# Sample keys of the stick-breaking attention: 14 of 32 unit products moved from VectorE to GpSimd

## The chip, the cores and the metric

The kernel runs on one core of one Trainium2 chip. The metric is the device time of one execution in microseconds (us), lower is better. Engines are named TensorE (PE in the profile), VectorE (DVE), ScalarE (ACT), GpSimd (POOL) and SyncE (SP).

## The reference

One step of one hybrid decoder layer, for a prompt of 256 tokens and 8 sample tokens (one token for each of 8 sequences, each with 2048 tokens of paged past), all in float32, width 1024. The change touches one product of it: the sample queries of the stick-breaking attention with the past keys.

```
def _stick_breaking(q, k, v, q_pos):
    z = jnp.einsum('bqhd,bshd->bhqs', q, k).astype(jnp.float32) * HEAD_DIM ** -0.5
    strict = (jnp.arange(L)[None, :] < q_pos[:, None])[None, None]
    log_keep = jnp.where(strict, jax.nn.log_sigmoid(-z), 0.0)
    after = lax.cumsum(log_keep, axis=3, reverse=True) - log_keep
    a = jnp.where(strict, jnp.exp(jax.nn.log_sigmoid(z) + after), 0.0)
    o = jnp.einsum('bhqs,bshd->bqhd', a, v)
```

Here b is one of 8 samples, h one of 8 heads, s one of 2048 past positions, d one of 64 dimensions. Beside it runs a sparse attention (for each query the best 256 keys by an indexer's score, then softmax), then projections, gates, and a mixture of 32 experts.

## The kernel before, in words

The first third of the program is a mixture of four streams, each written out by hand in the order of one engine's queue; semaphores tie them together.

The key product. The 2048 past keys of a sample are cut into 4 units. A unit is 128 partitions x 4 positions x 512 numbers (8 heads x 64), 1 MB. There are 32 units, k = 0 to 31; b = k // 4 is the sample and u = k % 4 the slot of a ring of four (`k_ring`). For each unit VectorE does two things in `unit(k)`: a product of the unit with the sample's query, broadcast over the four positions, written in place (line 1536), and a sum over the 64 dimensions of each head into `z_s` (line 1540), which also frees the slot (`s_kused`). The query lies on all partitions in one of two buffers (`q_all[:, b % 2]`); SyncE loads those of samples 0 and 1, ScalarE the rest in `load_q(b)` (line 1208), each after the products of sample b - 2 are done (`s_mul`).

GpSimd's queue. It issues the gathers (indirect DMAs, line 506): first units 0 to 3 mixed with the indexer's keys and the first pair of `fetch_ka` (keys of the sparse attention), then in a loop over k = 4 to 31: wait until unit k - 4 is summed, fetch unit k. After k = 9, 15 and 17 it also waits for TensorE (`s_tr`) and issues the next pair of `fetch_ka`. Each pair is 2 fetches, for samples `pair` and `pair + 4`. After the loop it fetches the values (`fetch_v`), the first four of them again after units 28 to 31.

VectorE's queue. Units 0 to 8 with small work between them, then the search for the 256 best keys of the sparse attention in 16 rounds. Round i is `unit(9 + i)`, then `search_answer(i)` (it waits for TensorE's count i), then `search_ask(i + 1)` (it compares scores with three candidates, counts within a partition, and posts `s_cnt` for TensorE's `count_above(i + 1)`, line 583, which adds over partitions). `search_ask(0)` stands before round 0. After the rounds: `unit(25)`, `search_taken`, `unit(26)`, `softplus_keys(0)`, `unit(27)`, `masked_softmax`, `unit(28)`, `later_keys(0)`, units 29 to 31, and then `prompt_a_scores(0)` (line 1728), which needs TensorE's prompt scores after a relu on ScalarE (line 1310). At the end of this chain `inverse_sums` (line 1667) releases a transpose of TensorE (line 815).

TensorE's queue. Input projections in chunks of 128 columns (`chunk`, line 577), with the counts, transposes and scores of the sparse attention's sample keys (lines 698 and 711) between them: count 0, 2 chunks' work, count 1, and so on to count 15, then one more (lines 791 and 793) after the last round. Pair p of the sparse keys is turned as soon as its two fetches are in.

Of the kernel before, what the change touches and what calls it, by code (L numbers as in the profile page):

```python
# [17 lines left out]
ALU = mybir.AluOpType  # L18
# [3 lines left out]
P = 128  # L22
# [3 lines left out]
NS = 8  # L26
T = NP_TOK + NS
TILES = [(0, P), (P, P), (2 * P, NS)]
H = 8
HD = 64  # L30
# [89 lines left out]
def decoder_step(nc, a, out, CONST_AT):  # L120

    ctx = ExitStack()
    with ctx:
# [3 lines left out]
        def sem(name):  # L127
            return ctx.enter_context(nc.semaphore(name))
# [7 lines left out]
        def const(name):  # L136
            c, r, n = CONST_AT[name]
            return consts[0:r, c:c + n]
# [19 lines left out]
        k_ring = arena[:, 0:RING // 2].rearrange("p (u r n) -> p u r n", u=4, r=4)  # L158
# [79 lines left out]
        q_all = flat[:, 0:2 * 512].rearrange("p (s n) -> p s n", s=2)  # L238
# [31 lines left out]
        def piece(n):  # L270
# [59 lines left out]
        s_k = [sem(f"s_k{u}") for u in range(4)]  # L330
        s_v = [sem(f"s_v{u}") for u in range(8)]
        s_q = [sem(f"s_q{i}") for i in range(2)]
        s_qdram, s_mul, s_kused, s_ls, s_sps, s_scan, s_ts, s_as, s_vused, s_owide, s_apad0, s_apad1 = (
            sem(n) for n in ("s_qdram", "s_mul", "s_kused", "s_ls", "s_sps", "s_scan", "s_ts", "s_as", "s_vused",
                             "s_owide", "s_apad0", "s_apad1"))
        s_vaused, s_oas, s_wide = sem("s_vaused"), sem("s_oas"), sem("s_wide")

        s_wp, s_wo, s_gains, s_wr, s_pab, s_mixa, s_mix = (sem(n) for n in (
# [46 lines left out]
        WEXP, NEWREL = PS[:, 0, 264:272], PS[:, 0, 272:288]  # L385
        COUNT = [PS[:, 1 if 2 <= i < 8 else ACC + 3, 0:3 * NS] for i in range(ROUNDS)]
        STRICT, UPTO = PS[:, ACC + 3, 24:32], PS[:, ACC + 3, 32:40]
        block = ctx.enter_context(nc.Block())

        @block.sync  # L390
# [111 lines left out]
        @block.gpsimd  # L502
        def _(pool):
            def fetch(dst, src, idx, landed):

                pool.indirect_dma_start(out=dst, out_offset=None, in_=src,  # L506
                                        in_offset=bass.IndirectOffsetOnAxis(ap=idx, axis=0)).then_inc(landed, 16)

            def fetch_k(k):
                b, u = k // 4, k % 4  # L510
                fetch(k_ring[:, u].rearrange("p r n -> p (r n)"), kb_rows, unit_idx[:, u, b:b + 1], s_k[u])

            def fetch_ka(pair):
                for which in range(2):
                    b = pair + 4 * which
                    fetch(ka_ring(pair, which), ka_rows, page_idx[:, b:b + 1], s_ka[pair % 2])

            pool.wait_ge(s_ms, 1)
            nc.gpsimd.tensor_tensor(rstd, ms, const("half"), ALU.pow).then_inc(s_rstd, 1)
            pool.wait_ge(s_idx, 4)  # L520
            pool.wait_ge(s_wa, 16)
            for g in range(2):
                for k in (2 * g, 2 * g + 1):
                    fetch_k(k)
                for b in range(4 * g, 4 * g + 4):
                    fetch(kidx_ring[:, b, :], kidx_rows, page_idx[:, b:b + 1], s_kidx[g])
            fetch_ka(0)
            for k in range(4, 4 * NS):
                pool.wait_ge(s_kused, k - 3)
                fetch_k(k)  # L530
                if k == 9:
                    pool.wait_ge(s_tr, M_KIDX + 8)
                    fetch_ka(1)
                if k == 15:
                    pool.wait_ge(s_tr, M_KA + 8)
                    fetch_ka(2)
                if k == 17:
                    pool.wait_ge(s_tr, M_KA + 16)
                    fetch_ka(3)

            def fetch_v(n):
                fetch(v_slot(n).rearrange("p r n -> p (r n)"), vb_rows, unit_idx[:, n % 4, n // 4:n // 4 + 1], s_v[n % 8])

            for n in range(4):
                pool.wait_ge(s_kused, 4 * NS - 3 + n)
                fetch_v(n)
            pool.wait_ge(s_proj, N_ALL)
            nc.gpsimd.memset(a_pads[0], 0.0).then_inc(s_apad0, 1)
            for n in range(4, 4 * NS):
                if n >= 8:  # L550
                    pool.wait_ge(s_vused, n - 7)
                fetch_v(n)
            for b in range(NS):
                if b < 4:
                    pool.wait_ge(s_vused, 4 * NS - 7 + b)
                else:
                    pool.wait_ge(s_vaused, b - 3)
                fetch(k_ring[:, b % 4].rearrange("p r n -> p (r n)"), va_rows, page_idx[:, b:b + 1], s_v[b % 4])

            for n, t in enumerate((0, 2, 1)):  # L560
                pool.wait_ge(s_ms2, n + 1)
                nc.gpsimd.tensor_tensor(rstd[:, t:t + 1], ms[:, t:t + 1], const("half")[:, t:t + 1], ALU.pow
                                        ).then_inc(s_rstd2, 1)

            for t in range(3):
                pool.wait_ge(s_ms3, t + 1)
                nc.gpsimd.tensor_tensor(rstd[:, t:t + 1], ms[:, t:t + 1], const("half")[:, t:t + 1], ALU.pow  # L567
                                        ).then_inc(s_rstd3, 1)

        @block.tensor  # L570
        def _(pe):
# [494 lines left out]
            def collect(i):  # L1066

                pe.wait_ge(s_into, i + 1)
                for half in range(2):
                    for t, (_, n) in enumerate(TILES):  # L1070
                        last = nc.tensor.matmul(PS[:, half, :], into[0:n, t, :], x2_rows[t][0:n, half * 512:(half + 1) * 512],  # L1071
                                                start=(t == 0), stop=(t == 2))
                    last.then_inc(s_xg, 1)
# [95 lines left out]
        def _(act):  # L1169
# [34 lines left out]
            act.wait_ge(s_qdram, 16)  # L1204

            def load_q(b):
                act.wait_ge(s_mul, 4 * (b - 1))
                act.dma_start(q_all[:, b % 2, :], q_dram[b:b + 1, :].to_broadcast([P, H * HD])).then_inc(s_q[b % 2], 16)

            def turned_kidx(j):  # L1210
# [10 lines left out]
            for j in range(2 * NS):  # L1221
                turned_kidx(j)
                if j in (6, 10, 14):
                    relu_kidx(j // 4 - 1)
            relu_kidx(3)
            load_q(2)

            for c in range(4):
# [260 lines left out]
        def _(dve):  # L1489
# [40 lines left out]

            def unit(k):
                b, u = k // 4, k % 4
                if u == 0:
                    dve.wait_ge(s_q[b % 2], 16 * (b // 2 + 1))
                dve.wait_ge(s_k[u], b * 16 + 16)
                nc.vector.tensor_tensor(k_ring[:, u], k_ring[:, u],  # L1536
                                        q_all[:, b % 2:b % 2 + 1, :].to_broadcast([P, 4, H * HD]), ALU.mult
                                        ).then_inc(s_mul, 1)
                dve.wait_ge(s_mul, k + 1)
                nc.vector.tensor_reduce(z_s[:, b, :].rearrange("p (h r) -> p r h", r=R)[:, 4 * u:4 * u + 4, :],  # L1540
                                        k_ring[:, u].rearrange("p r (h d) -> p r h d", h=H), AX_X, ALU.add
                                        ).then_inc(s_kused, 1)

            for k in range(3):
                unit(k)
# [541 lines left out]
```

## Time and profile before

| | before |
|---|---|
| time, median of 3 runs | 770.74 us (766.74 to 774.0) |
| profiled execution | 770.5 us, of which the span is 768.7 |
| mean granted TensorE clock | 0.891 |
| TensorE busy | 624.5 us, 81% |
| VectorE busy | 377.3 us, 49% |
| ScalarE busy | 150.1 us, 20% |
| GpSimd busy | 110.4 us, 14% |

The span is the time from the first to the last instruction that the profile shows; the rest of the execution's time lies around it. Start times below are microseconds from the span's start. "Busy" leaves out waits, branches and the issuing of DMAs by queues; GpSimd's gathers count, since it works on them. The granted clock is a share of 2.4 GHz.

### The profile page before, as it was taken

Reading aid. Unit: us, or ns where it says so; the run is one execution under the profiler, and the core shown is the slowest. Engines: PE = TensorE matmul, PEld = TensorE weight load, DVE = VectorE, ACT = ScalarE, POOL = GpSimd, SP = SyncE. Lnnn points to the kernel's source line nnn. Section 1 sums busy time; section 2 is a strip of 40 time slices with the busy share of each in tenths; the row PEclk is TensorE's granted clock in tenths of the full one; section 3 lists DMA queues with packets and bytes.
Section 4 is the critical chain, followed back from the end, with each engine's and each line's share of the span. In section 5 each row is a group of like instructions: output and inputs, shape, how many; then the busy total and the mean of one; then the engine's idle time right before and its main releaser. Section 6 shows DMA issues by size and latency. Waiting matters only on the chain.

```text
span 768.7 us, 8533 instructions
## 1 busy us (share of the span) xinstructions
PE 624.5 (81%) x3304; PEld 350.2 (46%) x3304; DVE 377.3 (49%) x667; ACT 150.1 (20%) x283; POOL 110.4 (14%) x100
## 2 busy tenths in 40 slices
PE   3997899899899798886569997488797977979743
PEld 2874774487688554542358545232222312223111
DVE  3059999898699987032003234643231323313204
ACT  2124014403401451524100010021101101011001
POOL 2513514101012435112100000000000000000001
PEclk9998899999999879688859998599989989999976
DMA  9997987869873889956879490039999999999931
GB/s 334 411 408 277 383 298 305 324 216 365 319 269 123 301 322 384 373 192 255 351 245 405 157 349 0 1 107 376 398 401 387 404 392 397 404 385 404 393 142 57
DMA packets 116928, 230.89 MB, mean 300 GB/s; under 512 B 14235, under 2 KB 82347, under 8 KB 106620
## 3 DMA queue, kind: packets, MB, share of 16 engines
q1 hardware_dynamic: 100556, 138.23, 49.1%
q0 software_dynamic: 12672, 88.09, 29.5%
q10 hardware_dynamic: 3664, 4.10, 1.7%
q8 instruction: 23, 0.38, 0.2%
q14 instruction: 13, 0.11, 0.0%
HBM read 225.77 MB, written 4.61 MB: 300 GB/s over the span
## 4 chain that ended last, share of the span: by engine, by line
PE 39%; SPq 25%; DVE 16%; DMA 8%; ACT 6%; issue 5%; ACTq 1%; POOL 1%; DVEq 0%
SPq L437 22%; PE PS L577 9%; DVE arena L1536 4%; PE PS L995 4%; DVE x_rows L1540 4%; PE PS L1011 4%; PE PS L921 3%; SPq L441 3%; DMA arena<-in_cache_v_a,page_idx 2%; DMA arena<-in_w_down 2%; PE PS L1071 2%; PE PS L698 2%; DMA temp<-in_cache_k_a,page_idx 1%; PE PS L1087 1%; DMA x_rows<-q_dram 1%
## 5 line engine op out<-in xcount | busy, mean ns | idle before, releaser
L577 PE MATMUL PS<-xT,arena 128*128 128x264 f32 x608 | 142.7, 394 | 3.8 <-ACT arena L1318 3.5
L577 PEld LDWEIGHTS PS<-xT,arena 128*128 128x128 f32 x608 | 116.2, 194 | 25.3 <-ACT arena L1318 4.0
L1087 PE MATMUL PS<-arena,temp 128*32 128x512 f32 x512 | 70.9, 704 | 29.0 <-DMA arena<-in_w_up 26.7
L1536 DVE TENSOR_TENSOR arena<-arena,x_rows 128x2048 f32<-128x2048 f32 x32 | 73.1, 2283 | 29.1 <-DMA x_rows<-q_dram 29.0
L1540 DVE TENSOR_REDUCE x_rows<-arena 128x32 f32<-128x2048 f32 x32 | 73.2, 2288 | 1.1
L1986 DVE TENSOR_TENSOR x_rows<-PS,x_rows 128x512 f32<-128x512 f32 (+1 forms) x48 | 33.0, 687 | 74.0 <-PE PS L1095 74.0
L506 POOL DMA_INDIRECT arena<-in_cache_k_b,unit_idx x32 | 39.4, 1230 | 145.2 <-DVE x_rows L1540 140.5
L1087 PEld LDWEIGHTS PS<-arena,temp 128*32 128x32 f32 x512 | 17.2, 126 | 80.4 <-issue 51.5
L1095 PE MATMUL PS<-temp 128*128 128x512 f32 (+1 forms) x96 | 47.4, 629 | 6.0 <-issue 6.0
L506 POOL DMA_INDIRECT arena<-in_cache_v_b,unit_idx x32 | 37.9, 1186 | 76.0 <-PE PS L921 55.4
L567 POOL TENSOR_TENSOR small<-small,consts 128x1 f32<-128x1 f32 x3 | 2.6, 867 | 289.2 <-DVE small L2038 289.2
L1135 PE MATMUL PS<-arena,temp 128*32 128x512 f32 x256 | 31.9, 643 | 12.9 <-ACT temp L1452 7.9
L1095 PEld LDWEIGHTS PS<-temp 128*128 128x128 f32 (+1 forms) x96 | 12.5, 161 | 41.1 <-DVE x_rows L1986 22.7
L2010 DVE COPY temp<-PS 128x512 f32<-128x512 f32 x8 | 5.5, 691 | 49.3 <-PE PS L1135 49.3
L1011 PE MATMUL PS<-temp,xT 128*128 128x512 f32 x64 | 28.0, 596 | 0.0
L1071 PE MATMUL PS<-rows_vb,temp 128*128 128x512 f32 x32 | 19.0, 676 | 8.2 <-DVE temp L1937 8.2
L1185 ACT COPY arena<-PS 128x264 f32<-128x264 f32 x22 | 8.3, 378 | 85.6 <-PE PS L577 85.6
L1438 ACT COPY temp<-PS 128x264 f32<-128x264 f32 x8 | 3.0, 378 | 103.0 <-PE PS L1102 102.9
L1135 PEld LDWEIGHTS PS<-arena,temp 128*32 128x32 f32 x256 | 8.3, 117 | 30.9 <-issue 29.6
L1241 ACT COPY temp<-PS 128x512 f32<-128x512 f32 x32 | 17.4, 588 | 22.7 <-PE PS L698 22.7
L937 PE MATMUL PS<-arena,temp 128*32 128x128 f32 x256 | 11.4, 347 | 12.6 <-DMA arena<-in_cache_v_a,page_idx 12.6
L1957 DVE COPY temp<-PS 128x512 f32<-128x512 f32 x8 | 5.5, 691 | 29.2 <-PE PS L1071 29.2
(338 smaller groups left out, 855.4 us busy)
## 6 DMA issues: line engine op xcount, KB each, us to landing
arena<-in_w_gate SPq DMA_DIRECT2D x64, 512.0 KB, 7.1
arena<-in_w_up SPq DMA_DIRECT2D x64, 512.0 KB, 7.7
arena<-in_w_down SPq DMA_DIRECT2D x32, 1024.0 KB, 10.5
arena<-in_w_in SPq DMA_DIRECT2D x9, 2048.0 KB, 11.6
temp<-in_w_out SPq DMA_DIRECT2D x1, 4096.0 KB, 15.2
x_rows<-in_x_prompt SPq DMA_DIRECT2D x2, 1024.0 KB
bias_dram<-x_rows SPq DMA_DIRECT2D x1, 2048.0 KB, 17.4
arena<-in_w_proj_a SPq DMA_DIRECT2D x1, 2048.0 KB, 9.4
```

What stands on the lines that cost most here:

```text
L437: sp.dma_start(both[:, chunks, g, :], w[e].rearrange("o (p c) f -> (o p) c f", p=P)[:, chunks, :]).then_inc(s_we[half], 16)
L506: pool.indirect_dma_start(out=dst, out_offset=None, in_=src, in_offset=bass.IndirectOffsetOnAxis(ap=idx, axis=0)).then_inc(landed, 16)
L577: last = nc.tensor.matmul(PS[0:m, n % 2, 0:T], w[:, k, c0:c0 + m], xT[:, k, :], start=(k == 0), stop=(k == KC - 1))
L995: last = nc.tensor.matmul(PS[:, bank + c % 2, 0:T], w[:, k, c * P:(c + 1) * P], o[:, k, :], start=(k == 0), stop=(k == 3))
L1011: last = nc.tensor.matmul(PS[:, (6 + 2 * t + n) % 8, :], mixT[:, k, t * P:(t + 1) * P], w_o[:, k, n * 512:(n + 1) * 512], start=(k == 0), ...
L1071: last = nc.tensor.matmul(PS[:, half, :], into[0:n, t, :], x2_rows[t][0:n, half * 512:(half + 1) * 512], start=(t == 0), stop=(t == 2))
L1087: last = nc.tensor.matmul(PS[k * CAP:(k + 1) * CAP, 2, :], xgT[:, d, k * CAP:(k + 1) * CAP], slots[k][:, d * 2 * DE:(d + 1) * 2 * DE], sta ...
L1095: return nc.tensor.matmul(PS[0:n, ACC + 2 + half, :], backT[:, t0:t0 + n], y_sb[:, half, :], start=True, stop=True)
L1135: last = nc.tensor.matmul(PS[k * CAP:(k + 1) * CAP, ACC + half, :], hidT[:, f, k * CAP:(k + 1) * CAP], slots[k][:, w0:w0 + 512], start=(f ...
L1536: nc.vector.tensor_tensor(k_ring[:, u], k_ring[:, u], q_all[:, b % 2:b % 2 + 1, :].to_broadcast([P, 4, H * HD]), ALU.mult).then_inc(s_mul, 1)
L1540: nc.vector.tensor_reduce(z_s[:, b, :].rearrange("p (h r) -> p r h", r=R)[:, 4 * u:4 * u + 4, :], k_ring[:, u].rearrange("p r (h d) -> p r ...
L1986: nc.vector.tensor_tensor(x_rows[0:n, t, cols], PS[0:n, ACC + 2 + half, :], x_rows[0:n, t, cols], ALU.add).then_inc(added, 1)
```

## The change

Units 5, 7, 9, ... 31 (14 of 32) have their product made on GpSimd; their sums stay on VectorE, as do both steps of the other 18 units. The product is the same operation on the same tiles. GpSimd makes the product of unit k - 2 right after it has issued the fetch of unit k, so its loop is: wait for the sum of unit k - 4, fetch unit k, and for odd k from 7 on wait for the query and for unit k - 2's data, multiply, post `s_mulp`. The fetches of the sparse keys after k = 9, 15 and 17 come behind that product. The last product, of unit 31, follows the loop and waits for the sum of unit 28. VectorE waits for `s_mulp` in the place of the product. `load_q(b)` waits for both counts of products.

```diff
+        def on_pool(k):
+            return k >= 5 and k % 2 == 1
+        def pool_products(k):
+            return sum(on_pool(j) for j in range(k))
+        def key_product(engine, k):
+            b, u = k // 4, k % 4
+            return engine.tensor_tensor(k_ring[:, u], k_ring[:, u], q_all[:, b % 2:b % 2 + 1, :].to_broadcast([P, 4, H * HD]),
+                                        ALU.mult)
...
+            def multiply(k):
+                b, u = k // 4, k % 4
+                if on_pool(k):
+                    pool.wait_ge(s_q[b % 2], 16 * (b // 2 + 1))
+                    pool.wait_ge(s_k[u], b * 16 + 16)
+                    key_product(nc.gpsimd, k).then_inc(s_mulp, 1)
+
             for k in range(4, 4 * NS):
                 pool.wait_ge(s_kused, k - 3)
                 fetch_k(k)
+                multiply(k - 2)
                 if k == 9:
                     pool.wait_ge(s_tr, M_KIDX + 8)
                     fetch_ka(1)
...
+            pool.wait_ge(s_kused, 4 * NS - 3)
+            multiply(4 * NS - 1)
...
             def load_q(b):
-                act.wait_ge(s_mul, 4 * (b - 1))
+                act.wait_ge(s_mul, 4 * (b - 1) - pool_products(4 * (b - 1)))
+                if pool_products(4 * (b - 1)):
+                    act.wait_ge(s_mulp, pool_products(4 * (b - 1)))
...
             def unit(k):
                 b, u = k // 4, k % 4
-                if u == 0:
-                    dve.wait_ge(s_q[b % 2], 16 * (b // 2 + 1))
-                dve.wait_ge(s_k[u], b * 16 + 16)
-                nc.vector.tensor_tensor(k_ring[:, u], k_ring[:, u],
-                                        q_all[:, b % 2:b % 2 + 1, :].to_broadcast([P, 4, H * HD]), ALU.mult
-                                        ).then_inc(s_mul, 1)
-                dve.wait_ge(s_mul, k + 1)
+                dve.wait_ge(s_q[b % 2], 16 * (b // 2 + 1))
+                if on_pool(k):
+                    dve.wait_ge(s_mulp, pool_products(k + 1))
+                else:
+                    dve.wait_ge(s_k[u], b * 16 + 16)
+                    key_product(nc.vector, k).then_inc(s_mul, 1)
+                    dve.wait_ge(s_mul, k + 1 - pool_products(k))
                 nc.vector.tensor_reduce(z_s[:, b, :].rearrange("p (h r) -> p r h", r=R)[:, 4 * u:4 * u + 4, :],
```

## Rows read from the trace of the kernel before

**Rows 1.** The page, chain that ended last: shares of the span by engine and line.

```profile
PE 39%; SPq 25%; DVE 16%; DMA 8%; ACT 6%; issue 5%; ACTq 1%; POOL 1%; DVEq 0%
SPq L437 22%; PE PS L577 9%; DVE arena L1536 4%; PE PS L995 4%; DVE x_rows L1540 4%; PE PS L1011 4%; PE PS L921 3%; SPq L441 3%; DMA arena<-in_cache_v_a,page_idx 2%; DMA arena<-in_w_down 2%; PE PS L1071 2%; PE PS L698 2%; DMA temp<-in_cache_k_a,page_idx 1%; PE PS L1087 1%; DMA x_rows<-q_dram 1%
```

**Rows 2.** Table by stretches: start:end, length, busy time (x instructions), clock, DMA.

```profile
core 0: us, PE busy (x) PEld busy (x) DVE busy (x) ACT busy (x) POOL busy (x), PEclk, DMA share, GB/s
67.00:92.00 25.00, 21.23 (x126) 15.36 (x124) 24.61 (x20) 7.50 (x15) 14.36 (x8) 0.91 0.78 281
...
151.00:187.00 36.00, 34.64 (x169) 28.36 (x169) 32.36 (x41) 7.71 (x19) 4.68 (x5) 1.00 0.74 269
...
213.50:254.00 40.50, 40.50 (x208) 34.44 (x207) 39.11 (x37) 6.17 (x16) 9.55 (x6) 1.00 0.55 188
254.00:267.00 13.00, 7.51 (x49) 6.01 (x47) 12.09 (x38) 6.13 (x10) 6.52 (x6) 0.84 0.84 307
```

**Rows 3.** Timeline of VectorE, 67 to 92 us: start, length, operation.

```profile
71.76 2.28 DVE L1536 TENSOR_TENSOR arena<-arena,x_rows 128x2048 f32<-128x2048 f32 x1
74.08 2.29 DVE L1540 TENSOR_REDUCE x_rows<-arena 128x32 f32<-128x2048 f32 x1
76.28 2.28 DVE L1536 TENSOR_TENSOR arena<-arena,x_rows 128x2048 f32<-128x2048 f32 x1
```

**Rows 4.** Timeline of ScalarE and VectorE at the end of the units.

```profile
248.22 0.60 ACT L1310 ACTIVATE temp<-PS 128x512 f32<-128x512 f32 x1 [0.73 <-PE PS L777]
...
253.80 0.47 DVE L1728 SCALAR_TENSOR_TENSOR temp<-temp,stat_p,consts 128x256 f32<-128x256 f32 x1
```

**Rows 5.** Timeline of TensorE; in brackets its idle time before, and the releaser.

```profile
92.37 0.62 PE L583 MATMUL PS<-temp,consts 128*128 128x24 f32 x2 [2.52 <-DVE temp L1594]
...
142.01 1.09 PE L698 MATMUL PS<-consts,temp 128*128 128x128 f32 x8 [1.28 <-DMA temp<-in_cache_k_a,page_idx]
...
158.81 0.30 PE L583 MATMUL PS<-temp,consts 128*128 128x24 f32 x2
...
173.50 0.30 PE L583 MATMUL PS<-temp,consts 128*128 128x24 f32 x2
...
266.88 0.27 PE L815 MATMUL PS<-consts,pads 64*8 64x64 f32 x1 [4.21 <-DVE pads L1667]
```

**Rows 6.** Timeline of GpSimd: a small product and its memset.

```profile
11.52 0.86 POOL L519 TENSOR_TENSOR small<-small,consts 128x3 f32<-128x3 f32 x1 [11.06 <-DVE small L1514]
...
257.34 1.83 POOL L548 MEMSET xT<- 128x2080 f32 x1 [2.24 <-PE PS L577]
```

**Rows 7.** DMA issues by line; the last number is us from issue to landing.

```profile
arena<-in_cache_k_b,unit_idx POOLq DMA_INDIRECT x32, 8.3
```

**Rows 8.** Timeline of GpSimd: fetches of units, and the last fetch of the sparse keys.

```profile
61.11 0.94 POOL L506 DMA_INDIRECT arena<-in_cache_k_b,unit_idx  x1 [1.79 <-DVE x_rows L1540]
...
72.11 2.74 POOL L506 DMA_INDIRECT arena<-in_cache_k_b,unit_idx  x1 [4.74 <-DVE x_rows L1540]
76.63 2.74 POOL L506 DMA_INDIRECT arena<-in_cache_k_b,unit_idx  x1 [1.78 <-DVE x_rows L1540]
...
130.44 0.93 POOL L506 DMA_INDIRECT temp<-in_cache_k_a,page_idx  x1 [0.30 <-issue]
```

**Rows 9.** Timeline of VectorE, first and next after the search's small work.

```profile
111.66 0.17 DVE L1600 TENSOR_SCALAR temp<-PS 128x24 f32<-128x24 f32 x1
...
113.61 2.28 DVE L1536 TENSOR_TENSOR arena<-arena,x_rows 128x2048 f32<-128x2048 f32 x1
```

**Rows 10.** Chain that ended last, in order of time: start, length, what.

```profile
130.44 11.53 DMA temp<-in_cache_k_a,page_idx
```

**Rows 11.** Table by stretches around the wait at 266.88 us; clock before the last two columns.

```profile
254.00:261.00 7.00, 6.17 (x31) 4.80 (x29) 6.51 (x18) 3.80 (x5) 4.14 (x4) 1.00 0.74 284
...
267.00:279.00 12.00, 12.00 (x45) 5.85 (x44) 10.55 (x15) 9.68 (x26) 3.65 (x3) 0.50 0.90 350
...
285.00:291.00 6.00, 6.00 (x48) 3.28 (x48) 5.56 (x19) 0.70 (x2) 2.02 (x3) 1.00 1.00 381
```

More of the change, by code:

```diff
@@ L335, in decoder_step @@
                              "s_owide", "s_apad0", "s_apad1"))
+        s_mulp = sem("s_mulp")
         s_vaused, s_oas, s_wide = sem("s_vaused"), sem("s_oas"), sem("s_wide")
```

## The prediction

> **What bounds the kernel now.** The page's chain of waits comes first [rows 1]: matrix work, SyncE's weight loads and VectorE share the path. The two VectorE lines of this change, the product L1536 and the sum L1540, carry 4.4% and 3.9% of it, 64 us together, while 32 units of 2.28 + 2.29 us [rows 3] keep VectorE busy for 146: more than half of them is hidden. The table by stretches [rows 2] says where. From 67 to 92 us and from 213.5 to 267 VectorE is full (24.61 of 25, 39.11 of 40.5, 12.09 of 13). From 151 to 187 TensorE is full (34.64 of 36) and VectorE, with its search rounds between the units, merely nearly so (32.36). The reader should see that a saving on VectorE is worth something before its first question to TensorE (count 0, at 92.37 us, waited 2.52 us for it [rows 5]) and after its last (from 214 on), and next to nothing between, where every count is answered by a TensorE that has other work. Of the 32 units the stretch before 92 us holds 5 and 7 of the moved ones, the middle holds 9 to 25, the tail 27, 29 and 31. After 267 us nothing of the change runs; all later weight loads wait for TensorE's steps, so I carry a shift at 267 us to the end one to one.
>
> **What is removed.** 14 products of 2.28 us leave VectorE, 31.9 us in all; from one product's start to the next a unit takes 4.52 us (71.76 to 76.28), an odd unit now 2.2. On the path are only five of them: 5 and 7, worth 4.6 us, and 27, 29, 31, worth 6.8. This is the most that the change could bring there, 11.4 us, and the tail can't give all of its share: VectorE's next work, the prompt's scores from 253.80 us, needs TensorE's scores after ScalarE's relu, whose first part ends at 248.82 [rows 4], so the tail is worth at most 4.9 us; at its end TensorE idled 4.21 us for VectorE [rows 5], which caps it at 4.2.
>
> **What is added on GpSimd.** One product of 128x2048 with two SBUF inputs. The trace has no such row. Below it lies VectorE's own 2.28 us [rows 3]. GpSimd's memset of 128x2080 took 1.83 us with one pass over the elements, and its product of 128x3 took 0.86 us, nearly all fixed cost [rows 6]. Three passes (two reads, one write) and the fixed part give 3 x 1.83 + 0.86 = 6.4 us, the other end; with the write overlapping the reads it is 2 x 1.83 + 0.86 = 4.5 us. I take 4.5, since an engine that streams would overlap its writes, and keep 2.3 and 6.4 for the range. The Trainium skill, page GPSIMD Engine Reference, section Elementwise — side-by-side cycle accounting, gives 4497 ns for a tensor_tensor addition of 2048 float32 elements, against 2293 on VectorE; the latter agrees with the 2.28 here, the former no row shows, and the sum would be the same by it.
>
> **What is moved: the order on GpSimd.** Its queue is strict. In the new loop, fetch k is followed by the product of unit k-2, and then, after k = 9, 15 and 17, come the second to fourth pairs of key fetches for the other attention. So the product of unit 7 stands ahead of the second pair, 13 ahead of the third and 15 ahead of the last, and each product waits for its data too. A unit lands 8.3 us after its issue [rows 7]; in the walk below unit 7 is fetched at 66.4 and multiplied at 79.6, so waits for landings add at most a few tenths. The waits added on ScalarE (the query loads for samples 3 to 7 now wait for GpSimd's products as well) are for products of the sample before the last, done some 10 us earlier, and cost nothing; were one late, ScalarE's evacuations behind it would hold TensorE up.
>
> **The two engines together.** A fetch whose issue falls in a VectorE product takes 2.74 us: those of 72.11 and 76.63 [rows 8] end 0.8 us after the products that began at 71.76 and 76.28 [rows 3]. Where VectorE runs a sum or a small operation it takes 0.94, as at 61.11. So a VectorE operation with two SBUF inputs shuts GpSimd out for its whole length. Whether a GpSimd product shuts VectorE out in the same way no row shows: the fetches are too short, and the memset reads nothing. Bounds for each meeting: nothing, or what is left of GpSimd's 4.5 us. I take the full exclusion, because the block in the other direction is for a whole instruction. The Trainium skill, page SBUF — State Buffer, section Who interferes with whom, says that a VectorE instruction with two SBUF inputs and a GpSimd one that reads SBUF exclude each other for a whole instruction, whichever starts first; by that the sum stays as below, without it the first rival holds. The same section has it that such a product doesn't hold up a GpSimd-issued transfer; the 2.74 us here say that it does.
>
> **The walk.** Rules: fetch 0.30 + 0.94 us, or until 0.8 after the VectorE product it meets; GpSimd product 0.30 + 4.5 us; VectorE product 2.3, sum 2.2; whoever has two SBUF inputs and comes second waits. Walked through the kernel before, without the change, the same rules give its counts and its end of the units within 0.4 us.
> Start to count 0. Units 4 and 5: GpSimd waits for product 4, multiplies 69.5 to 74.0, the sum of 5 ends at 76.3 as before: 0 instead of -2.3. Units 6 and 7: the fetch meets product 6 (3.1 us), then 4.5 us, then the sum of 7: 10.1 us instead of 9.0, +1.1. Unit 8 is alone and VectorE reaches the first question's comparison (two inputs) about 1 us into GpSimd's product of unit 9: it waits 3.6 us. Count 0 is late by 1.1 + 3.6 = 4.7 us.
> Counts 0 to 16. After an odd unit's sum come small search operations of 2 us (111.66 to 113.61 [rows 9]), by which time GpSimd has fetched (1.24) and begun a product; VectorE's even product waits until 6.0, runs with its sum to 10.6, 2 us of search, the sum of the odd unit: 14.7 us a pair, against 2 x (4.5 + 2.0) = 13.0 before. TensorE takes 14.7 us for a pair of counts from 151 us on (158.81 to 173.50 [rows 5]), so no more is lost there, but nothing is to spare. Its counts 3 to 5 are closer together, and there VectorE costs it another 1 us, which the wait for the third key pair hides again but for 0.2. Until count 6 the shift is +4.9.
> The last key pair. Its second fetch was issued at 130.44 [rows 8] and was in 11.53 us later, at 141.97 [rows 10]; TensorE took it up at 142.01, having waited 1.28 us [rows 5]. Now fetch 17 comes at 130.2, product 15 from 131.4 to 135.9, and the first of the two fetches meets VectorE's product of unit 14 (2.7 us): the second is issued at 139.3, 8.8 us later. TensorE's shift becomes +9.1 us at count 7, and it stays so through the TensorE-bound stage.
> Tail. The operations after the last count wait for product 27 (+2.4), odd units give 3 x -2.3 = -6.8, unit 28 waits 0.8 for product 29 and unit 30 1.2 for product 31: -2.4. The end of the units and TensorE's first dependent step at 267 us are late by 9.1 - 2.3 = about 6.9 us.
> The clock. TensorE stood for 4.2 us before 266.88, and from 267 to 279 it was granted 0.50, its 1.2 GHz level; before (254 to 261) and after (285 to 291) it had 1.00 [rows 11]. New idle of 4.7 us before count 0 and some 4 us more before the last key pair invite the same; the wait at 267 shrinks to 2 us, which may spare it. From half to all of 6 us of lost work each: I put +2 for the three together, with -4 and +8 as ends.
> Sum: profiled execution 770.5 us (span 768.7 and 1.8 outside; the median of the runs is 770.74) + 6.9 + 2 = about 779 us.
>
> **Rivals.** (a) GpSimd's product doesn't hold VectorE. For it: the trace shows only the other direction. Then, with 4.5 us, count 0 is on time (-0.1), count 7 is late by 1.3 us through the last key pair, and the tail pays back 4.2: -2.9 at 267 us, and the wait before 266.88 and its slow 12 us go too, up to -6 more at the clock. 762 to 768 us. It needs only that VectorE's products stay 2.3 us long while GpSimd multiplies. (b) The exclusion holds and the product is short, 3.5 us or less. By the same walk with 3.5 us, 267 us is on time; with 2.3, count 0 is 1.9 early, count 7 1.5, and the tail gives 4.1: -5.6. So 765 to 772. (c) It holds and the product is long. From 5 us on the pair of rounds on VectorE exceeds TensorE's 14.7 us, so each pair of the middle costs as well as the start and the tail. The walk with 5.5 us has count 0 late by 7.7, count 16 by 17 and 267 us by 19; with 6.4 us it is 10, 26 and 31. So 784 to 802. (d) The ring of four slots is refilled later, by up to 4.5 us for each GpSimd product, and the engines wait for landings. With landings after 10 us instead of 8.3 the walk comes out the same, so I give this little: 1 to 3 us on top of the forecast, 780 to 789.
>
> **How the numbers follow.** Forecast 0.45 (773 to 786), (a) 0.20, (b) 0.13, (c) 0.17, (d) 0.05. The range of 766 to 793 leaves out half of (a), a part of (b) and the upper half of (c), about 2 in 10. 1% of 770.7 is 7.7 us, about what a measurement of this kernel can tell from no change: below 763 lies a third of (a) and nothing else to speak of, 0.07; above 778.4 lie (c) and somewhat over half of the forecast and a part of (d), 0.50; between, 0.43.
>
> **What the profile after would show.** GpSimd has 14 products of about 4.5 us. VectorE's even products meeting them show as stretched or preceded by waits of up to 4 us (for the forecast) or as plain 2.28 us (for a). Count 0 comes near 97 us (92 for a), the last key pair's second fetch near 139 us, count 16 near 222, the last sum ends near 260. A product of GpSimd with another length than 4.5 makes me wrong first; a shift that is right at 267 us and not at the end would put the fault in the later stages, the clock above all.

## The result and the profile after

The changed kernel takes 786.78 us (median of 4, 783.52 to 789.7) against 769.24 for the kernel before: ratio 1.0219, 95% interval 1.0148 to 1.0291, so 2.2% slower. The loss is clear of the noise; whether it is more or less than 2% is not. The profiled execution is 784.76 us long, its span 782.9 us, 14.2 more than before. In what follows the product line L1536 has become L398 (the helper `key_product`), the sum L1540 is L1567, and lines below the change on VectorE have moved by 27, on TensorE by 25. Where an experiment adds or removes lines of its own they move a little further: L1624 of e2 is L1619 of the changed kernel, L1568 of e3 is L1567.

From the page of the changed kernel: busy time by engine, the chain that ended last, and three of the costliest groups (busy, mean ns, then idle before).

```profile
PE 630.3 (81%) x3304; PEld 353.1 (45%) x3304; DVE 398.2 (51%) x653; ACT 150.3 (19%) x283; POOL 169.1 (22%) x114
...
PE 30%; DVE 27%; SPq 24%; issue 6%; DMA 6%; ACT 4%; POOL 1%; DVEq 0%; POOLq 0%; ACTq 0%
...
L398 POOL TENSOR_TENSOR arena<-arena,x_rows 128x2048 f32<-128x2048 f32 x14 | 63.3, 4525 | 5.1 <-DVE x_rows L1567 4.8
L398 DVE TENSOR_TENSOR arena<-arena,x_rows 128x2048 f32<-128x2048 f32 x18 | 41.1, 2283 | 29.0 <-DMA x_rows<-q_dram 29.0
L1619 DVE TENSOR_TENSOR temp<-temp 128x408 f32<-128x408 f32 x16 | 38.5, 2409 | 0.6
```

VectorE's share of the chain went from 16% [rows 1] to 27%. Its busy time should have fallen by 14 x 2.28 = 31.9 us, from 377.3 to 345.4; it is 398.2. So 52.8 us of "busy" on VectorE is time in which an instruction had begun and stood still, and GpSimd's 14 products last 63.3 us. The products on VectorE keep their 2283 ns. What grew is L1619, the search's comparison of 128x408, which has two SBUF inputs: 2409 ns on average against the 583 it takes when nothing holds it. Six of its 16 executions took 5.4 to 5.5 us, the other ten 0.58.

First the plain lengths, from the timeline of VectorE in the kernel before (start, length):

```profile
66.97 0.41 DVE L1565 TENSOR_SCALAR pads<-pads 128x8 f32<-128x8 f32 x2
67.24 2.28 DVE L1536 TENSOR_TENSOR arena<-arena,x_rows 128x2048 f32<-128x2048 f32 x1
...
125.44 0.58 DVE L1592 TENSOR_TENSOR temp<-temp 128x408 f32<-128x408 f32 x1
...
238.59 0.69 DVE L1693 TENSOR_TENSOR x_rows<-x_rows,small 128x512 f32<-128x512 f32 x1
```

The timeline of VectorE in the changed kernel:

```profile
67.30 5.16 DVE L1592 TENSOR_SCALAR pads<-pads 128x8 f32<-128x8 f32 x2
72.37 2.28 DVE L398 TENSOR_TENSOR arena<-arena,x_rows 128x2048 f32<-128x2048 f32 x1
...
86.82 2.29 DVE L1567 TENSOR_REDUCE x_rows<-arena 128x32 f32<-128x2048 f32 x1 [3.13 <-POOL arena L398]
...
94.61 3.31 DVE L1616 TENSOR_TENSOR temp<-search_steps,bound_s 128x24 int32<-128x24 int32 x1
...
102.09 5.04 DVE L1637 TENSOR_SCALAR digit_i<-digit_i 128x8 int32<-128x8 int32 x1
...
119.55 5.45 DVE L1619 TENSOR_TENSOR temp<-temp 128x408 f32<-128x408 f32 x1
...
229.37 4.01 DVE L1657 TENSOR_TENSOR temp<-temp 128x136 f32<-128x136 f32 x1
...
255.58 5.00 DVE L1720 TENSOR_TENSOR x_rows<-x_rows,small 128x512 f32<-128x512 f32 x1
```

and that of GpSimd in the same kernel:

```profile
66.77 0.94 POOL L519 DMA_INDIRECT arena<-in_cache_k_b,unit_idx  x1 [4.39 <-DVE x_rows L1567]
67.74 4.55 POOL L398 TENSOR_TENSOR arena<-arena,x_rows 128x2048 f32<-128x2048 f32 x1
...
120.02 4.53 POOL L398 TENSOR_TENSOR arena<-arena,x_rows 128x2048 f32<-128x2048 f32 x1
...
228.71 4.51 POOL L398 TENSOR_TENSOR arena<-arena,x_rows 128x2048 f32<-128x2048 f32 x1
...
255.51 4.52 POOL L398 TENSOR_TENSOR arena<-arena,x_rows 128x2048 f32<-128x2048 f32 x1 [4.83 <-DVE x_rows L1567]
```

Read them in pairs. GpSimd's product of 120.02 ends at 124.55; VectorE's comparison, begun at 119.55, ends at 125.00 and not at 120.13. The same with 228.71 and L1657, and with 255.51 and L1720, which begins 0.07 us after the product. GpSimd's product begins 0.03 us after the end of its fetch (66.77 + 0.94 to 67.74), and the first of them holds a small operation with one tensor input (L1592) too.

The order of the recorded starts doesn't tell who wins. The comparison of 119.55 began 0.47 us before GpSimd's product, and still stood. When the product ended at 124.55 it needed another 0.45 of its 0.58 us, so it had stopped about 0.34 us before the recorded start of the product (an estimate from these rows). L1592 is another such case: both of its instructions would have been over by 67.71, and the product is recorded from 67.74.

The timeline of TensorE in the changed kernel, its counts and the step at the end of VectorE's chain (idle time and releaser in brackets):

```profile
99.21 0.62 PE L608 MATMUL PS<-temp,consts 128*128 128x24 f32 x2 [8.12 <-DVE temp L1621]
...
125.67 0.40 PE L608 MATMUL PS<-temp,consts 128*128 128x24 f32 x2 [0.90 <-DVE temp L1621]
...
156.63 0.40 PE L608 MATMUL PS<-temp,consts 128*128 128x24 f32 x2 [2.22 <-DVE temp L1621]
...
203.54 10.30 PE L602 MATMUL PS<-xT,arena 128*128 128x264 f32 x32
...
283.54 0.27 PE L840 MATMUL PS<-consts,pads 64*8 64x64 f32 x1 [6.00 <-DVE pads L1694]
```

Against [rows 5]: count 0 at 99.21 and not 92.37, and the last step at 283.54, not 266.88, 16.7 us late. Between these TensorE waits again and again for the question (L1621), which before it did at count 0 alone: its waits for it before counts 1 to 15 add up to 8.2 us. The table by stretches of the changed kernel shows the middle against [rows 2]: VectorE has 35.21 of 36 us where it had 32.36, TensorE 32.41 where it had 34.64.

```profile
151.00:187.00 36.00, 32.41 (x154) 23.74 (x152) 35.21 (x32) 8.30 (x17) 17.40 (x7) 0.95 0.53 186
```

To compare kernels I cut each profiled execution at four marks of its trace: VectorE's first product (47.2 us before; it starts when the first query lands, which moves by up to 1.7 us from one execution to another), count 0, TensorE's last count (count 16), and the transpose that VectorE's chain releases (L815 before). All in us, the last column to the end of the span:

| kernel | first product to count 0 | to count 16 | to L815's step | to the end | ratio of times (95% interval) |
|---|---|---|---|---|---|
| before | 45.2 | 121.1 | 53.4 | 501.8 | 1 |
| changed | 51.7 | 129.2 | 55.2 | 499.4 | 1.0219 (1.0148 to 1.0291) |
| e1 products left out | 44.4 | 121.8 | 49.5 | 501.5 | 0.9931 (0.9891 to 0.9972) |
| e2 writes only | 44.3 | 119.2 | 50.6 | 506.8 | 0.9959 (0.9918 to 1.0) |
| e3 gated | 49.5 | 121.3 | 53.4 | 500.9 | 1.0067 (1.0026 to 1.0108) |
| e4 keys first | 53.2 | 127.7 | 56.5 | 503.6 | 1.0214 (1.0146 to 1.0282) |
| e5 units 5, 7 only | 46.0 | 122.9 | 53.5 | 501.4 | 1.0049 (1.0014 to 1.0084) |
| e6 units 9 to 25 only | 47.1 | 128.1 | 53.5 | 502.2 | 1.0126 (1.0078 to 1.0175) |
| e7 units 27, 29, 31 only | 45.2 | 122.8 | 55.5 | 508.7 | 1.0056 (1.0025 to 1.0087) |
| e8 units 27, 29, placed | 45.2 | 121.4 | 49.6 | 502.2 | 0.9992 (0.9958 to 1.0026) |
| e9 left out, query earlier | 42.6 | 116.6 | 49.5 | 502.8 | 0.9896 (0.9839 to 0.9953) |
| e10 gated, not 9 | 46.4 | 120.9 | 53.5 | 497.8 | 1.003 (1.0003 to 1.0056) |

The last column varies by several us among kernels that are the same there, so the three columns before it carry the reasoning and the ratios the verdicts. The second column has some play too: e7 changes nothing up to count 16 and shows 122.8 against 121.1, so differences below 2 us in it are not read.

### The profile page after: what moved, and what is told of

Same layout as the page of the kernel before. It is cut to its first block, busy times and chain, and to the rows that moved or that the text cites. A ratio compares the mean times of both kernels' runs of the same rounds, so it can differ in the third digit from the quotient of the medians.

```text
span 782.9 us, 8574 instructions
## 1 busy us (share of the span) xinstructions
PE 630.3 (81%) x3304; PEld 353.1 (45%) x3304; DVE 398.2 (51%) x653; ACT 150.3 (19%) x283; POOL 169.1 (22%) x114
## 4 chain that ended last, share of the span: by engine, by line
PE 30%; DVE 27%; SPq 24%; issue 6%; DMA 6%; ACT 4%; POOL 1%; DVEq 0%; POOLq 0%; ACTq 0%
SPq L450 21%; DVE x_rows L1567 6%; PE PS L602 5%; DVE temp L1619 5%; DVE arena L398 4%; PE PS L1020 4%; PE PS L1036 4%; PE PS L946 3%; SPq L454 3%; DMA arena<-in_cache_v_a,page_idx 2%; DMA arena<-in_w_down 2%; PE PS L1096 2%; PE PS L882 1%; PE PS L1112 1%; ACT temp L1378 1%
## 5 line engine op out<-in xcount | busy, mean ns | idle before, releaser
L602 PE MATMUL PS<-xT,arena 128*128 128x264 f32 x608 | 148.5, 406 | 0.3 <-DVE xT L1555 0.3
L602 PEld LDWEIGHTS PS<-xT,arena 128*128 128x128 f32 x608 | 120.6, 201 | 23.2 <-issue 1.3
L1567 DVE TENSOR_REDUCE x_rows<-arena 128x32 f32<-128x2048 f32 x32 | 72.9, 2284 | 3.8 <-POOL arena L398 3.1
L398 POOL TENSOR_TENSOR arena<-arena,x_rows 128x2048 f32<-128x2048 f32 x14 | 63.3, 4525 | 5.1 <-DVE x_rows L1567 4.8
L398 DVE TENSOR_TENSOR arena<-arena,x_rows 128x2048 f32<-128x2048 f32 x18 | 41.1, 2283 | 29.0 <-DMA x_rows<-q_dram 29.0
L1120 PE MATMUL PS<-temp 128*128 128x512 f32 (+1 forms) x96 | 47.2, 628 | 4.8 <-issue 4.8
L519 POOL DMA_INDIRECT arena<-in_cache_v_b,unit_idx x32 | 36.0, 1126 | 63.8 <-PE PS L946 54.7
L1619 DVE TENSOR_TENSOR temp<-temp 128x408 f32<-128x408 f32 x16 | 38.5, 2409 | 0.6
L2037 DVE COPY temp<-PS 128x512 f32<-128x512 f32 x8 | 5.5, 691 | 48.6 <-PE PS L1160 48.6
L1268 ACT COPY temp<-PS 128x512 f32<-128x512 f32 x32 | 17.5, 588 | 27.6 <-PE PS L723 27.6
```

The source lines that it names most:

```text
L398: return engine.tensor_tensor(k_ring[:, u], k_ring[:, u], q_all[:, b % 2:b % 2 + 1, :].to_broadcast([P, 4, H * HD]), ALU.mult)
L519: pool.indirect_dma_start(out=dst, out_offset=None, in_=src, in_offset=bass.IndirectOffsetOnAxis(ap=idx, axis=0)).then_inc(landed, 16)
L602: last = nc.tensor.matmul(PS[0:m, n % 2, 0:T], w[:, k, c0:c0 + m], xT[:, k, :], start=(k == 0), stop=(k == KC - 1))
L1120: return nc.tensor.matmul(PS[0:n, ACC + 2 + half, :], backT[:, t0:t0 + n], y_sb[:, half, :], start=True, stop=True)
L1619: link(nc.vector.tensor_tensor(above, score_s.unsqueeze(1).to_broadcast([P, 3, NS, RW]), cand_s.unsqueeze(3).to_broadcast([P, 3, NS, RW]), ...
```

## The experiments

Theory S: GpSimd's product, while it reads, holds VectorE. Theory Q: it costs by the room it takes in GpSimd's queue, ahead of fetches.

**e1, the moved products left out.** An upper bound of the gain, and a check of VectorE's altered waits alone.

```diff
-                    key_product(nc.gpsimd, k).then_inc(s_mulp, 1)
...
                 if on_pool(k):
-                    dve.wait_ge(s_mulp, pool_products(k + 1))
+                    dve.wait_ge(s_k[u], b * 16 + 16)
```

(and ScalarE's wait for `s_mulp` goes). Expected: 

> Leaves out the 14 moved products altogether (the odd units' sums are of the bare keys). It prices the removal alone: by the prediction's step on what is removed, count 0 comes some 4.5 us earlier than before (near 88 us), the counts between stay TensorE's, and the wait before TensorE's step at 267 us goes: 8 to 9 us off there and up to 6 more from the clock, so 755 to 762 us. If the change's loss came from something other than GpSimd's products (the altered waits on VectorE and ScalarE), this kernel would be slower than before too, near 785.

Measured: 0.7% faster, less than the 1 to 2% expected. The tail gave 53.4 - 49.5 = 3.9 us of its cap of 4.2. The first stretch gave 0.8 us and not 4.5. The timeline of VectorE in e1 says why:

```profile
85.92 2.29 DVE L398 TENSOR_TENSOR arena<-arena,x_rows 128x2048 f32<-128x2048 f32 x1 [3.80 <-DMA x_rows<-q_dram]
```

Unit 8 is the first that needs sample 2's query, and VectorE, early for once, stood 3.80 us for it. In the kernel before that load was just in time and hidden.

**e2, writes only.** GpSimd fills the unit with zeros two and a half times in place of the product (the odd units' products are left out).

```diff
-                    key_product(nc.gpsimd, k).then_inc(s_mulp, 1)
+                    n = pool_products(k)
+                    nc.gpsimd.memset(k_ring[:, u], 0.0).then_inc(s_fill, 1)
+                    pool.wait_ge(s_fill, 2 * n + 1)
+                    nc.gpsimd.memset(k_ring[:, u], 0.0).then_inc(s_fill, 1)
+                    pool.wait_ge(s_fill, 2 * n + 2)
+                    nc.gpsimd.memset(k_ring[:, u, 0:2], 0.0).then_inc(s_mulp, 1)
```

Expected: 

> GpSimd fills the unit with zeros two and a half times in place of multiplying (about 4.5 us in the same place of its queue, writes only, no reads; the odd units' products are left out). Theory S, GpSimd's reads shut VectorE out: with none, VectorE's operations keep their lengths, count 0 is near 92 us, the step at 267 us comes 3 us earlier than before, and the time is 762 to 768 us. Theory Q, the loss is the room that the products take in GpSimd's queue (later fetches, later key pairs): as the change, 783 to 790 us, count 0 near 99.

Measured: ratio 0.9959, median 766.92, as S had it; Q's 783 to 790 is ruled out. The altered waits on VectorE and ScalarE are all in this kernel, so they aren't the cause either. The timelines of GpSimd

```profile
90.42 1.82 POOL L548 MEMSET arena<- 128x2048 f32 x1
92.30 1.80 POOL L550 MEMSET arena<- 128x2048 f32 x1
94.16 0.95 POOL L552 MEMSET arena<- 128x1024 f32 x1
```

and of VectorE in the same kernel:

```profile
68.59 2.29 DVE L1597 TENSOR_SCALAR pads<-pads 128x8 f32<-128x8 f32 x2
68.86 2.29 DVE L398 TENSOR_TENSOR arena<-arena,x_rows 128x2048 f32<-128x2048 f32 x1
...
91.90 0.58 DVE L1624 TENSOR_TENSOR temp<-temp 128x408 f32<-128x408 f32 x1
...
237.73 1.95 DVE L1750 COPY arena<-arena 64x264 f32<-64x264 f32 x1
```

GpSimd is as long at work (90.42 to 95.11) as with a product, in the same place, and the comparison in the midst of it takes its plain 0.58 us. So the room taken in GpSimd's queue costs no time here by itself. Some operations with one tensor input do stretch beside a memset: two TENSOR_SCALARs take 2.29 us for 0.41, though the product behind them begins in time and keeps its length, and a copy of 64x264 near the end takes 1.95 us for 0.29, and what follows it waits.

**e3, gated.** Each GpSimd product begins only after VectorE's product of the unit before it, beside a sum.

```diff
+                    pool.wait_ge(s_mul, k - pool_products(k))
                     key_product(nc.gpsimd, k).then_inc(s_mulp, 1)
```

Expected: 

> The change with one wait more: GpSimd begins the product of unit j only when VectorE has finished the product of unit j - 1, so that it runs beside a sum (one SBUF input). Theory S: the first 2.2 us of each are free, the other 2.3 hold VectorE or are waited for, which is just what the moved product cost before: 767 to 775 us, count 0 near 92 to 95. Theory Q: the queue is as full as in the change and its fetches are later still, 785 us or more.

Measured: ratio 1.0067, median 776.4, just above S's range and far from Q's: with later products the loss falls to a third. The middle (121.3) and the tail (53.4) are the kernel before to 0.2 us, with all 14 products on GpSimd. What is left is in the first stretch. The timeline of VectorE in e3:

```profile
75.94 2.29 DVE L1568 TENSOR_REDUCE x_rows<-arena 128x32 f32<-128x2048 f32 x1 [2.49 <-POOL arena L398]
...
93.67 3.32 DVE L1617 TENSOR_TENSOR temp<-search_steps,bound_s 128x24 int32<-128x24 int32 x1
```

The sum of unit 5 waits 2.49 us for its product: some 2.2 us of 4.5 were free beside a sum, the rest costs what the moved product had cost (2.28). Unit 9's product still falls on the first question (3.32 for 0.18).

**e10, gated, with unit 9's product back on VectorE.**

```diff
-            return k >= 5 and k % 2 == 1
+            return k >= 5 and k % 2 == 1 and k != 9
```

Expected: 

> The gated kernel (a GpSimd product starts only after VectorE's product of the unit before) with unit 9's product left on VectorE. In the gated kernel the first question's first operation was held 3.3 us by product 9, its only large loss at count 0 (49.5 us from the first product against 45.2). Theory S: 46 us here, the rest as in the gated kernel, so about 3 us less than it and 1 to 2 us over the kernel before: 771 to 774 us. If the 4.3 us were the price of products 5 and 7, it stays at 49.

Measured: 46.4 us to count 0, 3.1 less than e3, ratio 1.003. Thirteen of the 14 products on GpSimd, placed in this way, cost 0.3% and gain nothing.

**e4, sparse keys first.** In each turn of GpSimd's loop the product comes last.

```diff
                 fetch_k(k)
-                multiply(k - 2)
...
                     fetch_ka(3)
+                multiply(k - 2)
```

Expected: 

> The change with the fetches of the sparse keys put ahead of the product in each turn of the loop. The prediction's step on the last key pair had it cost 4.2 us: then this kernel is about 4 us faster than the change, 780 to 784 us. Theory S, by the trace after: TensorE found the last pair in place and waited for VectorE's questions instead, so within 2 us of the change, 784 to 789 us.

Measured: 1.0214 against the change's 1.0219, no gain. The timeline of TensorE in e4 just after the last pair is taken up:

```profile
152.54 1.09 PE L723 MATMUL PS<-consts,temp 128*128 128x128 f32 x8
...
158.47 0.40 PE L608 MATMUL PS<-temp,consts 128*128 128x24 f32 x2 [2.47 <-DVE temp L1621]
```

It doesn't wait for the pair at all, but for VectorE's next question. The changed kernel shows the same, in its own timeline of TensorE:

```profile
147.87 0.40 PE L608 MATMUL PS<-temp,consts 128*128 128x24 f32 x2
...
150.96 1.09 PE L723 MATMUL PS<-consts,temp 128*128 128x128 f32 x8
```

This row is the better proof, since e4 issued the last fetch of the pair only 0.5 us earlier than the changed kernel (141.15 against 141.66): the run alone says little on what an early pair would be worth.

**e5, e6, e7: the parts.** Only the set of units differs from the change.

```diff
-            return k >= 5 and k % 2 == 1
+            return k in (5, 7)                    # e5
+            return 9 <= k <= 25 and k % 2 == 1    # e6
+            return k in (27, 29, 31)              # e7
```

Expected of e5: 

> Only units 5 and 7 on GpSimd. By the trace after, count 0 was 6.8 us late with unit 9's product in the way of the first question (3.3 us of it). Theory S: count 0 late by about 3.5 us, the same at 267 us, 771 to 776 us. Theory Q with no shutting out gives 0 there.

Expected of e6: 

> Only units 9 to 25 on GpSimd. Theory S: 3.3 us at count 0, then a pair of rounds on VectorE of 15.5 us against TensorE's 14.7, so some 11 us late at count 16 and at 267 us: 778 to 783 us. If the middle were TensorE's and without cost, as the prediction had it from 151 us on, about 5 us late: 774.

Expected of e7: 

> Only units 27, 29 and 31 on GpSimd. The prediction's tail gives 2.4 us back: 766 to 768 us. The trace after had the tail 1.8 us longer (17's hold of 3.7 after the last count, 4.3 on the update of later keys, 0.7, against 6.8 saved): 770 to 773 us.

Measured: +0.5%, +1.3% and +0.6%, together 2.3% against 2.2% for the whole, so the loss is spread over all parts, most of it in the middle. Count 0 is later by 0.8 us in e5, not by 3.5, and by 1.9 in e6, while both sets together cost 6.5. A race decides the difference. The timeline of GpSimd in e5:

```profile
67.49 0.94 POOL L519 DMA_INDIRECT arena<-in_cache_k_b,unit_idx  x1 [4.40 <-DVE x_rows L1567]
68.45 6.52 POOL L398 TENSOR_TENSOR arena<-arena,x_rows 128x2048 f32<-128x2048 f32 x1
```

and of VectorE:

```profile
68.02 0.41 DVE L1592 TENSOR_SCALAR pads<-pads 128x8 f32<-128x8 f32 x2
68.29 2.28 DVE L398 TENSOR_TENSOR arena<-arena,x_rows 128x2048 f32<-128x2048 f32 x1
```

Here VectorE's product of unit 4 went through, and GpSimd's stood for it: 6.52 us and not 4.5. In the changed kernel GpSimd's went through, held L1592 and with it VectorE's product until 72.37, 4.8 us later than before when counted from the first product. L1592 is recorded 0.43 us ahead of GpSimd's product in e5 and 0.44 ahead in the changed kernel, so about a hundredth in the records separates the two outcomes, and the same code gives either. e7's tail is 2.1 us longer than before, as in the changed kernel (1.8).

**e8, units 27 and 29 only, placed where VectorE can't be held for long.**

```diff
-            return k >= 5 and k % 2 == 1
+            return k in (27, 29)
...
-                multiply(k - 2)
+                if k == 28:
+                    multiply(27)
+                if k == 31:
+                    multiply(29)
```

Expected: 

> Only units 27 and 29 on GpSimd, where VectorE has little with two SBUF inputs: 27 right after fetch 28, while VectorE waits for TensorE's count 15 (4.7 us before), 29 after fetch 31, beside the masked softmax (4.6 us with one SBUF input each). Theory S: each saves 2.2 us and holds VectorE for under 1, so the step at 267 us is 3 to 4 us earlier, 764 to 767 us; were it enough that a product is on GpSimd at all to lose time, 770 or more.

Measured: the tail is 49.6 us, 3.8 less than before and the same as with the products left out: TensorE's step no longer waits for VectorE. The timelines in e8, of GpSimd,

```profile
203.65 4.52 POOL L398 TENSOR_TENSOR arena<-arena,x_rows 128x2048 f32<-128x2048 f32 x1
...
228.60 4.54 POOL L398 TENSOR_TENSOR arena<-arena,x_rows 128x2048 f32<-128x2048 f32 x1
```

of VectorE,

```profile
232.29 0.87 DVE L1689 TENSOR_TENSOR pads<-pads 64x1 f32<-64x1 f32 x1
```

and of TensorE:

```profile
264.09 0.22 PE L843 MATMUL PS<-consts,pads 64*8 64x64 f32 x1 [0.39 <-ACT temp L1369]
```

Each product saves 2.28 us and holds VectorE for under a microsecond (L1689 takes 0.15 us otherwise). Yet the ratio is 0.9992 (0.9958 to 1.0026): 3.8 us would be 0.5%, just outside. So the gain at the mark is shown, a gain in the whole time is not.

**e9, the products left out and sample 2's query loaded earlier.**

```diff
             for j in range(2 * NS):
                 turned_kidx(j)
+                if j == 11:
+                    load_q(2)
...
             relu_kidx(3)
-            load_q(2)
```

Expected: 

> The kernel with the 14 products left out, and ScalarE's load of sample 2's query (needed from unit 8 on) issued after the twelfth of 16 evacuations of the indexer's keys and not after the last. In the first left-out kernel VectorE reached unit 8 early and stood 3.80 us for that query, so that count 0 came only 0.8 us earlier from the first product on. If the query's load is what caps the first stretch, the stretch from first product to count 0 falls from 44.4 us to between 42.5 and 43 (TensorE's own work ends 2.5 us before count 0 in the kernel before, which is the next bound); if not, it stays at 44.4.

Measured: 42.6 us to count 0, 1.8 less than e1, and VectorE's 3.80 us are gone: the query's load was the cap, and TensorE's own work is the next one. The ratio is 0.9896, though of two executions only. Why the middle is 4.5 us shorter than before (116.6) wasn't tried; in e9 TensorE's clock was 1.00 from 92 to 102 us, where the kernel before had 0.83.

## Why the prediction was right, and where its sum was short

The direction, slower, came out, and so did its cause; the size was put at +8.9 us (6.9 and 2) on the profiled execution and is +14.3 (+17.5 between the medians).

**The product's price.** 4.5 us from GpSimd's memset and its small product; 4525 ns measured. The figure of the Trainium skill (page GPSIMD Engine Reference, section Elementwise — side-by-side cycle accounting), 4497 ns, agrees with it within 1%.

**The exclusion.** Right, and the trace after shows the direction that the trace before could not (52.8 us of VectorE standing). Rival (a), no hold on VectorE, is out; e2 is what it would have been: 0.9959, not the 1% or so at its optimistic end. An operation was stretched in either order (5.45 us for 0.58 on VectorE; 6.52 for 4.5 on GpSimd). By the rule of the Trainium skill, page SBUF — State Buffer, section Who interferes with whom, it would be so, and the traces agree that the two exclude each other.

**What the moved products were worth.** "5 and 7, worth 4.6 us": wrong. [rows 5] already had TensorE only 2.52 us idle before count 0, and behind that lay a query load; e1 got 0.8. The tail's cap of 4.2 was right (3.9 in e1, 3.8 in e8).

**Start to count 0.** +4.7 forecast, +6.5 measured. The rule gave GpSimd 0.30 us between a fetch and a product; the trace has 0.03. So the product of unit 5 came before VectorE's product of unit 4 and not after, though by very little, as e5 shows: which of the two it is hangs on a few hundredths of a microsecond, and the trace before couldn't tell it. And "whoever has two SBUF inputs" was too narrow: TENSOR_SCALARs of 128x8 with one tensor input were held as well (5.16 for 0.41, and 5.04 for 0.17).

**Counts 0 to 16.** This is the mis-sized step: +4.4 forecast, of which only 0.2 for VectorE's late questions and 4.2 for the last key pair; +8.1 measured, with the pair costing nothing (next paragraph). The same 0.3 us: the walk let VectorE's small search work finish and ask before the product held it at the next big product. In fact VectorE never got that far: the comparison L1619 was caught in six rounds and a small operation before it in the two others with a GpSimd product, so each time the question itself went out 3 to 5 us late. From one GpSimd product to the next (181.96 to 197.44) a pair of rounds took 15.5 us, not 14.7, above TensorE's 14.7, and each question late made TensorE idle. TensorE's 8.2 us of waiting for questions before counts 1 to 15 are about the whole of the 8.1. e6 has this part alone: +7.0.

**The last key pair.** "+9.1 us at count 7" by the pair's late fetch: wrong as a cause. The last fetch was later than forecast (141.66 against 139.3), but TensorE was later still: count 6, put at +4.9 against before, is 10.3 us late (147.87 for 137.57), and the pair is then taken up without a wait at 150.96. At count 7 the forecast's +9.1 stands against 11.2, so the two are near each other by luck. The prediction took for a bound what another, larger delay had covered.

**Tail.** -2.3 forecast, +1.8 measured. The hold after the last count was seen (2.4 forecast, 3.7 measured, L1657). The product of unit 31, released by the sum of unit 28, fell on L1720, which begins 0.2 us after that sum; the walk had it begin behind that operation, through its 0.30 us again. These 4.3 us more (5.00 for 0.69) are the largest part of what turned the sign.

**The clock.** +2 was put as a balance of three places. Behind count 0, one of the places, the granted clock was 0.61 from 99 to 105 us, after TensorE had stood for 8.12 us; but the kernel before had 0.72 from 92 to 98. Behind the last key pair, the second, there is hardly a slow stretch (0.91 from 150 to 160). The third, the wait for VectorE's last step, grew to 6.00 us and didn't shrink to 2, and yet the clock behind it was 0.64 for 7 us (and 0.72 once more, from 296 to 302) where the kernel before had 0.50 for 12. One stretch stands where none was named: at 203.54, after 1.42 us without work, 32 matmuls of L602 took 10.30 us, which take 7.37 at 187.85 in the same kernel, with a granted clock of 0.50, the 1.2 GHz level, from 203 to 208. None of this was isolated, and the balance stays open.

**Rival (d)**, landings of units: VectorE's sum waited for GpSimd's product (3.13 us at unit 7), never for a unit's landing.

## What to carry to other kernels

Where two engines shut each other out, moved work doesn't leave: count for each moved operation the part that runs beside instructions which can't be held (here sums of 2.2 us), and charge the rest of its length to the engine that it was meant to relieve. A 2.28 us product made in 4.5 us elsewhere, beside one such sum, was worth nothing (e3's middle, e10), in the way of a short question to a third engine it costs up to its full length (the change), and beside idle time or a sum alone it gives back what it saves at the next mark (e8). Before such a move, look in the trace for everything that the other engine has under way where the new instruction will start, and don't count on an operation being safe because it is recorded first: here one recorded 0.47 us ahead was caught. And read the bound behind the first one, since e1 needs no second engine to show how little there was to win.

## What the runs showed of the hardware

GpSimd's gathers, when issued inside VectorE's two-input product, stand for it: 0.94 us become 2.74 [rows 8]. The one of 61.11, issued 0.44 us ahead of a product, keeps its 0.94. The Trainium skill, page SBUF — State Buffer, section Who interferes with whom, has it that such a product leaves transfers issued by GpSimd alone; the traces here differ. The exclusion takes single operations as small as 128x8 with one tensor input (TENSOR_SCALAR, 5.04 and 5.16 us), also beside a memset of GpSimd (2.29 us), which leaves a two-input comparison alone (0.58). A TENSOR_SCALAR that reads PSUM was not held in the midst of a GpSimd product (0.29 us at 93.69 in the changed kernel). The same section of the Trainium skill lists tensor_scalar among the operations that can take the shared ports in full, which agrees with both. Sums with one input were never held (2284 ns on average in the changed kernel, 2288 before). In these runs the order of the recorded starts doesn't tell which engine keeps the whole instruction: a VectorE comparison recorded 0.47 us ahead was caught, and a lead of 0.43 us in e5 and of 0.44 in the changed kernel ended one way and the other.
